# Conditioning weights: products on GpSimd in place of matrix products on TensorE

## The reference

```python
c_act = jax.nn.silu(c)                              # c: 1 x 1024
for l in range(2):
    mod = c_act @ ada_w[l] + ada_b[l]               # 1024 -> 6144 values, six vectors of 1024
    sh_m, sc_m, g_m, sh_f, sc_f, g_f = split(mod, 6)
    h = rmsnorm(x, norm_mix[l]) * (1 + sc_m) + sh_m
    proj = h @ w_in[l]                              # queries, keys, values, gates, ...
    # differential attention, latent attention, a state space branch: from proj
    x = x + g_m * (merged @ w_out[l])
    h = rmsnorm(x, norm_ffn[l]) * (1 + sc_f) + sh_f
    x = x + g_f * ffn(h)
```

## Time and profile before

| | us |
|---|---|
| median of 3 runs | 2510.01 (2509.58 to 2512.15) |
| the profiled execution | 2510.45 |
| its span | 2508.7 |
| TensorE busy | 2337.5 (93%) |
| VectorE busy | 1542.9 (62%) |
| ScalarE busy | 1092.7 (44%) |
| GpSimd busy | 59.9 (2%) |

### The profile page before, as it was taken

One profiled execution on the slowest core, in us unless ns is written; L12 is line 12 of the kernel. 1 busy time (PEld: TensorE's weight loads), 2 busy tenths in 40 slices (PEclk: granted clock), 3 DMA queues, 4 the chain that ended last, 5 costly groups with the idle time before them and its releaser, 6 DMA issues. The chain is left out here.

```text
span 2508.7 us, 37527 instructions
## 1 busy us (share of the span) xinstructions
PE 2337.5 (93%) x13974; PEld 1993.7 (79%) x13974; DVE 1542.9 (62%) x2861; ACT 1092.7 (44%) x1900; POOL 59.9 (2%) x73
## 2 busy tenths in 40 slices
PE   6999988999999999989999999978999999978998
PEld 3656776989976577778999899857997999857997
DVE  4796615667633572366776766773666666763765
ACT  2222334455533334254555544444544544444554
POOL 0000001200000000021000000000000000000000
PEclk9999998999999999999999999979999999979999
DMA  8754222444445523224544545203543445203552
GB/s 313 260 205 172 101 101 76 152 169 183 177 172 215 191 101 110 92 97 162 196 178 174 194 176 201 93 34 126 201 178 149 175 178 199 96 30 119 197 187 92
DMA packets 37540, 390.17 MB, mean 156 GB/s; under 512 B 4416, under 2 KB 5056, under 8 KB 5952
## 3 DMA queue, kind: packets, MB, share of 16 engines
q1 hardware_dynamic: 37440, 388.87, 41.8%
HBM read 387.80 MB, written 1.05 MB: 155 GB/s over the span
## 5 line engine op out<-in xcount | busy, mean ns | idle before, releaser
L1260 PE MATMUL bank<-h,ring 128*128 128x256 f32 x2048 | 477.6, 389 | 13.1 <-ACT h L1051 8.1
L1260 PEld LDWEIGHTS bank<-h,ring 128*128 128x128 f32 x2048 | 390.2, 193 | 103.9 <-issue 27.9
L689 DVE TENSOR_TENSOR ffn_w_lo<-ring,ffn_w_hi 128x2048 fp32r<-128x2048 f32 x126 | 288.8, 2292 | 165.4 <-ACT ffn_w_hi L638 165.3
L559 PE MATMUL bank<-ffn_hh,ffn_w_hi 128*128 128x512 f32 x1408 | 364.5, 400 | 13.1 <-DVE ffn_hh L819 11.1
L559 PEld LDWEIGHTS bank<-ffn_hh,ffn_w_hi 128*128 128x128 f32 x1408 | 258.5, 192 | 66.9 <-issue 9.7
L611 PE MATMUL bank<-ffn_g_hi,ffn_w_hi 128*128 128x256 f32 x1056 | 299.4, 284 | 6.1 <-DVE ffn_g_lo L734 6.1
L611 PE MATMUL bank<-ffn_g_lo,ffn_w_hi 128*128 128x256 f32 x1056 | 298.9, 283 | 0.0
L611 PE MATMUL bank<-ffn_g_hi,ffn_w_lo 128*128 128x256 f32 x1056 | 298.9, 283 | 0.0
L638 ACT ACTIVATE ffn_w_hi<-ring 128x2048 fp32r<-128x2048 f32 x126 | 239.7, 1902 | 0.8
L611 PEld LDWEIGHTS bank<-ffn_g_hi,ffn_w_hi 128*128 128x128 f32 x1056 | 202.8, 192 | 7.4 <-issue 7.4
L1417 ACT ACTIVATE work<-bank 128x256 f32<-128x256 f32 (+2 forms) x168 | 63.6, 380 | 325.4 <-PE bank L1260 319.9
(11 more groups left out here) (278 smaller groups left out, 3295.5 us busy)
## 6 DMA issues: line engine op xcount, KB each, us to landing
ring<-w_in SPq DMA_DIRECT2D x244, 1536.0 KB, 6.3
x<-x_in SPq DMA_DIRECT2D x1, 1024.0 KB, 15.3
mem<-mem_in SPq DMA_DIRECT2D x1, 1024.0 KB, 4.7
y_out<-x SPq DMA_DIRECT2D x4, 256.0 KB, 2.6
con<-con_in SPq DMA_DIRECT2D x1, 801.0 KB, 7.4
par<-par_in SPq DMA_DIRECT2D x2, 302.0 KB, 15.7
work<-pos_in SPq DMA_DIRECT2D x2, 128.0 KB, 6.2
par<-par_in SPq DMA_DIRECT2D x2, 76.0 KB, 4.6
```

The source lines that it names most:

```text
L559: pe.matmul(up_out(j, half, False), w_hi[:, j % 2, c0:c0 + P], hh[:, k, :, :], start=k == 0, stop=False)
L689: dve.tensor_tensor(w_lo[:, j % 2, UP], ring[:, (base + j) % RING, UP], w_hi[:, j % 2, UP], ALU.subtract).then_inc(S(tag + "_up_lo"), 1)
L1260: m = pe.matmul(ps[0:m_rows, 0:T], tile(t0 + k, base)[:, 0:m_rows], rhs, start=k == 0, stop=k == len(src) - 1 and kind != "uk")
```

## The change

The chunks of m1, m2 and n0 leave TensorE (`by_gpsimd`). GpSimd multiplies each chunk, 128 x 2048 numbers, by its column of c into SBUF (`tensor_scalar`), in two pieces where the chunk crosses a slot; for all but the first chunk of a pair it then adds the product to an accumulator of the same size (`tensor_tensor`). Once per pair a new step "adas" sums over the partitions on TensorE with four products of 512 columns and a matrix of ones; ScalarE copies the bank as before, and "adat" stays as it was. m0 stays on TensorE.

A slot may now be overwritten when TensorE has used its tiles and GpSimd has multiplied its chunks: the transfer waits for `tiles_used` and `tiles_summed`. The tiles of chunks are counted as used for TensorE with the next projection.

The chunks are dealt anew: 13 ahead of the attention in layer 0 and 9 in layer 1 (`ADA_EARLY`); the other 11 and 7 go into the attention, one for each of its first units. "adas" and "adat" stand some 24 tiles or two units behind a pair's last chunk. The bias steps of layer 0 still follow every second step of kind "proj" or "ada", from the fifth in place of the seventh.

```diff
+ADA_EARLY = (13, 9)
+def by_gpsimd(pair):
+    return pair != "m0"
+def column_steps(pair):
+    return [("adas", pair, 0), ("adat", pair, 0)]
@@ steps1a
-                while given < -(-len(chunks) * t // total):
-                    out += chunks[given]
+                while given < -(-early_chunks * t // total):
+                    out.append(chunks[given])
                     given += 1
+                    if given % KD == 0:
+                        due.append((t + 24, chunks[given - 1][1]))
...
+    units = [list(at) for at in AT1]
+    for u, c in enumerate(chunks[given:]):
+        units[u].append(c)
+        if c[2] == KD - 1:
+            units[u + 2] = column_steps(c[1]) + units[u + 2]
...
-                if n > 6 and n % 2 == 0 and rest:
+                if n > 4 and n % 2 == 0 and rest:
@@ first_half, SP and GpSimd
-                        stream_loop(sp, base + RING, base + plan.a_slots, S("tiles_used"), TPS, TPS)
+                        stream_loop(sp, base + RING, base + plan.a_slots, S("tiles_used"), TPS, TPS, S("tiles_summed"))
+                        for (pair, k), done in zip(plan.chunks, plan.pool_done):
+                            chunk_pool(pool, pair, k, done)
+                            if k == KD - 1:
+                                pool.wait_ge(S("ada_steps"), chunk_steps[pair, k] + steps_of((pair, k)))
+                                pool.nop().then_inc(S("ada_made"), 1)
@@ new
+            def chunk_pool(pool, pair, k, done):
+                n, ps = gp_index(pair), pieces(TILES1[pair, k], base)
+                if k:
+                    pool.wait_ge(S("ada_steps"), chunk_steps[pair, k])
+                if k == 1 and n:
+                    pool.wait_ge(S("tp_ready"), TSEQ["adas", gp_pairs[n - 1], 0] + 1)
+                acc_, prod = ada_acc[:, n % 2, :], ada_acc[:, 1 - n % 2, :]
+                for g, c0, cols, at in ps:
+                    pool.wait_ge(full[g % RING], 16 * (g // RING + 1))
+                    pool.tensor_scalar((prod if k else acc_)[:, at:at + cols], ring[:, g % RING, c0:c0 + cols],
+                                       cact[:, k, 0:1], None, ALU.mult).then_inc(S("ada_steps"), 1)
+                pool.wait_ge(S("ada_steps"), chunk_steps[pair, k] + len(ps))
+                slots_done(pool, done)
+                if k:
+                    pool.tensor_tensor(acc_, acc_, prod, ALU.add).then_inc(S("ada_steps"), 1)
@@ steps_pe
+                    if step == "ada" and by_gpsimd(kind):
+                        continue
+                    elif step == "adas":
+                        i, n = TSEQ[step, kind, j], gp_index(kind)
+                        pe.wait_ge(S("ada_made"), n + 1)
+                        if i >= 1:
+                            pe.wait_ge(S("tp_free"), i)
+                        for r in range(4):
+                            m = pe.matmul(bank[5][32 * r:32 * r + 32, :], ones[:, 0:32],
+                                          ada_acc[:, n % 2, 512 * r:512 * r + 512], start=True, stop=True,
+                                          skip_group_check=True)
```

More of the change, by code:

```diff
@@ L121, in steps1a @@
     pairs = ["m1", "m2"] + (["n0"] if layer + 1 < LAYERS else [])
-    chunks = [c for pair in pairs for c in [ada(pair, k) for k in range(KD)]]
-    chunks = [c + ([("adat", c[0][1], 0)] if c[0][2] == KD - 1 else []) for c in chunks]
+    chunks = [("ada", pair, k) for pair in pairs for k in range(KD)]
+    early_chunks = ADA_EARLY[layer]
     total = sum(WIDTH.get(s[1], 8) for s in steps if s[0] == "proj")
-    out, t, given = [], 0, 0
+    out, t, given, due = [], 0, 0, []
     for s in steps:
@@ L129, in steps1a @@
             t += WIDTH.get(s[1], 8)
+            if due and t >= due[0][0]:
+                out += column_steps(due.pop(0)[1])
             if t % 4 == 0:
-                while given < -(-len(chunks) * t // total):
-                    out += chunks[given]
+                while given < -(-early_chunks * t // total):
+                    out.append(chunks[given])
                     given += 1
-    assert given == len(chunks)
+                    if given % KD == 0:
+                        due.append((t + 24, chunks[given - 1][1]))
+    assert given == early_chunks
+    for _, pair in due:
+        out += column_steps(pair)
+    units = [list(at) for at in AT1]
[3 more added lines that the diff above has]
+            units[u + 2] = column_steps(c[1]) + units[u + 2]
     if layer == 0:
@@ L149, in steps1a @@
     return (out + [("pad", "", 4), ("vt", "va", 0), ("vt", "va", 1), ("vt", "vb", 0), ("vt", "vb", 1)]
-            + attention(16, AT1))
+            + attention(16, units))
+NOT_PE = ("", "m1", "m2", "n0")
 BUCKETS = 32
@@ L243, in used_marks @@
     marks, before = {}, first_tile
-    real = [b for b in blocks if b[0] != ""]
+    real = [b for b in blocks if b[0] not in NOT_PE]
     for kind, j, n in real:
@@ L274, in __init__ @@
         self.a_slots = max(self.tiles[kind, j][1] for step, kind, j in self.a if step in ("proj", "ada")) // TPS + RING
+        self.chunks = [s[1:] for s in order if s[0] == "ada" and by_gpsimd(s[1])]
+        firsts = [self.tiles[c][0] // TPS for c in self.chunks] + [self.a_slots]
+        self.pool_first, self.pool_done = firsts[0], [b - a for a, b in zip(firsts, firsts[1:])]
         self.nseq = {s[1:]: i for s, i in numbered(order, "sq").items()}
@@ L277, in __init__ @@
         self.aseq = {s[1]: i for s, i in numbered(order, "adat").items()}
-        turns = [s for s in order if s[0] in ("adat", "vt", "xt") or s == ("dt", "", 1)
+        turns = [s for s in order if s[0] in ("adas", "adat", "vt", "xt") or s == ("dt", "", 1)
                  or s[0] == "turn" and head_of(s[2]) is not None]
@@ L918, in mixer1 @@
             ropet, tmp256 = cut(512), cut(T)
+            ada_acc = cut(2 * 2048, (2, 2048))
             def p1(name, j=0, parts=slice(0, P)):
@@ L1142, in ada_pe, with slots_done, steps_of @@
                 m.then_inc(S("tiles_used"), USED1[pair, k][1])
+            gp_index = lambda pair: ASEQ[pair] - (layer == 0)
+            def slots_done(pool, n):
+                for _ in range(n):
+                    pool.nop().then_inc(S("tiles_summed"), TPS)
+            def chunk_pool(pool, pair, k, done):
[13 more added lines that the diff above has]
+                    pool.tensor_tensor(acc_, acc_, prod, ALU.add).then_inc(S("ada_steps"), 1)
+            def steps_of(c):
+                return len(pieces(TILES1[c], base)) + (c[1] > 0)
+            gp_pairs = [pair for pair, k in plan.chunks if k == 0]
+            chunk_steps = dict(zip(plan.chunks, np.cumsum([0] + [steps_of(c) for c in plan.chunks]).tolist()))
             def ada_of(pair):
@@ L1400, in steps_act @@
                         start_act(act, a)
-                    elif step == "adat":
+                    elif step == "adas":
+                        i, n = ASEQ[kind], TSEQ[step, kind, j]
+                        act.wait_ge(S("tp_ready"), n + 1)
+                        act.activation(rows[:, i % 2, :], bank[5][:, :], ACT.Copy).then_inc(S("tp_free"), 1)
+                        act.wait_ge(S("tp_free"), n + 1)
+                        act.nop().then_inc(S("ada_kept"), 1)
+                    elif step == "adat" and not by_gpsimd(kind):
                         i = ASEQ[kind]
```

7 lines of the change are left out of this document (6 added, 1 removed).

## The result

| | before | after |
|---|---|---|
| median, us | 2511.08 (2509.58 to 2516.64, 4 runs) | 2673.79 (2670.8 to 2675.67, 4 runs) |
| ratio, 95% interval | | 1.0638 (1.062 to 1.0655) |
| the profiled execution's span, us | 2508.7 | 2671.8 |

A forecast was written before the change was run, and what follows sets the result against it. TensorE was taken as the bound, with VectorE close behind and blocked by GpSimd's SBUF reads. Four first-block stretches, 34 + 49 + 35 + 9 = +127 us on 2510.45, gave 2637 us; eight in ten, 2570 to 2705.

The forecast's parts named there:

- The bound: Ahead of layer 0's attention, VectorE's 134.8 us plus GpSimd's 77 would outgrow TensorE's 178 us stretch, reaching 212.
- B: First eleven units of layer 0's attention: VectorE's 52.5 plus GpSimd's 68.5 gives 121 us against 72, +49.
- D: First seven units of layer 1's attention: VectorE's 31.8 plus GpSimd's 46.5 gives 78.3 us against 43, +35.
- C: Stretch of 164 us ahead of layer 1's attention: TensorE saves 8 us, stalled norms and ropes cost 17, +9.
- The multiplication: GpSimd's product of a 2048-column chunk, sized from the cast at 2.0 us, with 3.8 from the other side.
- the addition: GpSimd's addition of 2048 columns, taken as 4.65 us, the middle of 3.5 and 5.8.
- A: Stretch ahead of layer 0's attention: VectorE's 134.8 plus GpSimd's 77 gives 212 us against 178, +34.
- The exclusion: GpSimd instructions reading SBUF and VectorE operations with two SBUF inputs shut each other out for the whole instruction.
- Rival 1: GpSimd and VectorE slip past each other at little cost; GpSimd only keeps up with the ring: -22 us, 2488; 12%.
- Rival 2: Long GpSimd instructions let VectorE in between, or fall mostly into its idle time: half the loss, 2574 us; 12%.
- TensorE's relief: 40 chunks leave TensorE (40 us), five sums over partitions come in (5 us): -35 us if TensorE alone set the time.
- The sum: VectorE's queue costs its own time plus GpSimd's; the four stretches' 34 + 49 + 35 + 9 give +127 us, 2637.

## Why the prediction was right, and where it was not

**The bound.** Ahead of the first attention VectorE became the bound as forecast: busy for 95% of the stretch, with TensorE waiting for the read of the sums' bank. Without the reads of GpSimd (fills) all of this loss is gone. In the attentions (B and D) TensorE does wait for the probabilities, but there the forecast's mechanism isn't the only one. The fills, which leave VectorE's two-input operations alone, cost 46 and 33 us by GpSimd's pace and the waits of TENSOR_SCALAR (13 and 11 of these come with GpSimd idle). The forecast had no term for this, and in D its +35 was right by luck: +28 is measured, and the reads add nothing there. How much of B's +66 goes to each cause isn't parted, nor what TensorE's lower granted clock (0.77 and 0.87 there, 1.00 before) costs. The second halves and what follows kept their length. The forecast cut layer 1 at 883 us; that is the third unit's scores, and its first two stand at 877.4. By the table C and D together gave +42.2, where +9 and +35 had been forecast.

**The multiplication is the term that was mis-sized.** The prediction took 2.0 us for 2048 columns from the cast, with 3.8 as the upper end. It takes 5.44, beyond both ends. For VectorE 3.55 of these count, so the term to put in the sum was 3.6, not 2.0. With it, and 4.5 for the addition (the prediction's 4.65 was close): A 134.8 + 13 x 3.55 + 11 x 4.5 = 230 us, where the window has 233; B 52.5 + 11 x 3.55 + 10 x 4.5 = 137 against 135. By this sum the +55 and +66 in place of +34 and +49 are this term. But the agreement is better than the sum deserves. In A VectorE is busy 86 us longer, not the 96 of the holds, and 12 us idle; in B 58 longer, not 84, and 25 idle. In D the same sum gives 31.8 + 7 x 3.55 + 7 x 4.5 = 88, +45, where the whole attention grew by 28: with the right size the forecast there is further off. GpSimd was busy 449 us in place of 300 for the same reason.

**The exclusion** held as derived from two collisions. What was wrong in detail: a multiplication lets two-input operations in after 3.55 us, and the convolution's first operation L1634, counted as exempt, is not; nor is the comparison L1146. Rival 1 is out, since the bias operations grew to 0.978 us. Its 2488 is about what the kernel gives whose GpSimd only releases (2497); with GpSimd working for as long but reading nothing, and so without the exclusion, it is 2559. Rival 2's half of the loss is out for instructions of this length. It has something in it for shorter ones, since pieces of 512 columns took away a third of the loss.

**TensorE's relief** was said to be 35 us that hardly count, and 16 is measured. The 25 us that the new sums and chunks cost inside the attentions even with GpSimd idle weren't in the forecast; no run shows how much of them is left beside the other delays.

**The sum** of own time and time shut out comes near the kernel as it is, but is no law: it supposes that each hold is paid in full, and that VectorE never stands idle. Pieces let VectorE use the free part of every multiplication, and GpSimd pays for turns instead.

**What stays open:** why a multiplication lets VectorE in before its end. Two observations go together: the fills, which only write, hold a TENSOR_SCALAR of VectorE and no two-input operation, and a TENSOR_SCALAR waits for the multiplication's end, while a two-input operation is let in at 3.55. That the multiplication has done its reads by then would fit both, but no run shows it. Open too is why the repeated column costs 26 us. No version here that does the whole computation beats the kernel before; the chunks are better left to TensorE. By the estimate of 1.00 us each all 40 cost it 40 us, and with GpSimd doing nothing in their place only 16 were won.

## What to carry to other kernels

An idle GpSimd is not free: each of its instructions that reads SBUF stops VectorE's operations with two SBUF inputs, and even those that only write hold some of its TENSOR_SCALAR. So work moved to it has to be charged to VectorE, even where VectorE is busy only three quarters of the time (its share in the first attention before), and GpSimd's own pace has to be charged beside it: fills of the same length cost 61 us against a GpSimd that only releases. Measure the very operation before sizing it: for 2048 columns a cast and a multiplication by a scalar differ here by 2.7 times. If the work must be there, cut it in short pieces (56 us here). Then look at the sum that waits for it: TensorE waited 13.9 and 13.2 us there; whether a later place wins this back wasn't tried.

## What the hardware showed that was not expected

- TENSOR_SCALAR on GpSimd takes 5.44 us for 128 x 2048 float32 and 2.84 for 1024, with a column or a constant as factor; the cast of 1024 takes 1.09, the product with a repeated column 3.74 for 2048.
- It shuts a two-input operation of VectorE out for 3.55 of its 5.44 us but a TENSOR_SCALAR until its end; an addition shuts out both for its whole 4.5.
- Fills, which read nothing, leave two-input operations of VectorE alone (0.613) and delay a comparison with one input (a mean of 0.955 in place of 0.414).
- Cutting GpSimd's instructions to a quarter made it busy 80 us longer in all (529.6 against 449.2), VectorE 102 us shorter (1666.8 against 1768.4), and the kernel 56 us faster.
